# Residual block on one core: adaLN rows summed in two column halves, two stores moved later, S4's load moved ahead of the gate piece's

## The reference

```python
mod = silu(c) @ ada_w + ada_b                        # six rows of 1024: the adaLN rows
sh1, sc1, gt1, sh2, sc2, gt2 = split(mod, 6)
h = modulate(rmsnorm(x, pre_mix_g), sh1, sc1)
q_r, k_r, v_r, g_r, q_s, k_s, v_s, a_r, a_s = split(h @ w_in)
ret = silu(g_r) * groupnorm(retention(q_r, k_r, v_r, positions))   # 8 heads, chunks of 64 tokens
sb = stick_breaking(q_s, k_s, v_s)
mixed = sigmoid(a_r) * (ret @ w_ret_branch) + sigmoid(a_s) * (sb @ w_sb_branch)
x2 = x + gt1 * rmsnorm(mixed @ w_out, post_mix_g)
out = x2 + gt2 * rmsnorm(relu(modulate(rmsnorm(x2), sh2, sc2) @ w_ff1) ** 2 @ w_ff2)
```

## Time and profile before

| | us |
|---|---|
| runs, median (lowest to highest) | 1704.49 (1702.32 to 1706.66) |
| the profiled execution, own time | 1702.23 |
| its span | 1700.4 |
| TensorE busy | 1655.3 (97%) |
| DVE busy | 1048.7 (62%) |
| POOL busy | 753.5 (44%) |
| ACT busy | 661.6 (39%) |
| mean granted TensorE clock, 1 is full | 0.994 |

### The profile page before, as it was taken

The page is one execution under the profiler, slowest core; times in us unless marked ns, Lnnn a source line. Parts: engine busy times, 40 slices in busy tenths (PEclk is TensorE's granted clock), DMA queues, the critical chain, the costliest instruction groups (busy, mean ns, idle before and its releaser), DMA issues.

```text
span 1700.4 us, 25213 instructions
## 1 busy us (share of the span) xinstructions
PE 1655.3 (97%) x9680; PEld 1375.6 (81%) x9680; DVE 1048.7 (62%) x1350; ACT 661.6 (39%) x1130; POOL 753.5 (44%) x311
## 2 busy tenths in 40 slices
PE   5999999999998999999999999999999999999998
PEld 5887877777888898988888998787888888888876
DVE  6788788778346474942121557699664738383736
ACT  5566666210223243321001256435343444435352
POOL 2011111245534353523344752572767585858550
PEclk9999999999999999999999999999999999999999
DMA  9012121275835353423111444636684665748272
GB/s 355 21 70 81 41 85 65 93 280 194 337 125 213 137 188 114 152 100 149 50 49 49 162 166 157 222 137 231 244 330 172 272 239 217 285 166 341 99 293 99
DMA packets 62709, 288.32 MB, mean 170 GB/s; under 512 B 7956, under 2 KB 8852, under 8 KB 51992
## 3 DMA queue, kind: packets, MB, share of 16 engines
q1 hardware_dynamic: 50576, 258.57, 40.6%
q10 hardware_dynamic: 12040, 28.47, 4.6%
HBM read 249.25 MB, written 37.77 MB: 169 GB/s over the span
## 4 chain that ended last, share of the span: by engine, by line
PE 80%; DVE 9%; ACT 3%; issue 3%; DMA 3%; POOL 1%; SPq 0%; ACTq 0%; POOLq 0%; DVEq 0%
PE ps L872 8%; PE ps L874 8%; PE ps L873 7%; PE ps L1282 6%; PE ps L1284 6%; PE ps L1283 6%; PE ps L1327 4%; PE ps L1326 4%; PE ps L1325 4%; PE ps L958 4%; PE ps L959 4%; PE ps L960 4%; PE ps L1162 2%; PE ps L1011 2%; DVE fs_f L2388 2%
## 5 line engine op out<-in xcount | busy, mean ns | idle before, releaser
L1282 PE MATMUL ps<-w_hi,f_hi 128*128 128x512 f32 x440 | 175.3, 398 | 3.0 <-issue 2.7
L1284 PE MATMUL ps<-w_hi,f_lo 128*128 128x512 f32 x440 | 175.1, 398 | 0.0
L1283 PE MATMUL ps<-w_lo,f_hi 128*128 128x512 f32 x440 | 174.9, 397 | 0.0
L637 POOL TENSOR_TENSOR w_hi<-raw,zero 128x1024 fp32r<-128x1024 f32 x34 | 69.1, 2031 | 228.4 <-PE ps L874 113.4
L650 POOL TENSOR_TENSOR w_lo<-raw,w_hi 128x1024 fp32r<-128x1024 f32 x16 | 41.7, 2616 | 228.8 <-ACT w_hi L1405 202.1
L725 POOL TENSOR_TENSOR w_lo<-w,w_hi 128x1024 fp32r<-128x1024 f32 x34 | 84.7, 2496 | 112.2 <-ACT w_hi L1813 65.1
L1327 PE MATMUL ps<-ring,w_hi 128*128 128x512 f32 x336 | 134.0, 399 | 0.0
L1326 PE MATMUL ps<-ring,w_lo 128*128 128x512 f32 x336 | 132.4, 394 | 0.0
L1325 PE MATMUL ps<-ring,w_hi 128*128 128x512 f32 x336 | 131.8, 392 | 0.0
L2079 DVE TENSOR_TENSOR_SCAN uu<-uu 128x512 f32<-128x512 f32 (+7 forms) x96 | 100.0, 1083 | 37.5 <-ACT uu L1498 37.5
L667 POOL TENSOR_TENSOR w_lo<-raw,w_hi 128x1024 fp32r<-128x1024 f32 x24 | 59.7, 2492 | 132.6 <-ACT w_hi L1552 131.8
(11 more groups left out here) (300 smaller groups left out, 4801.4 us busy)
## 6 DMA issues: line engine op xcount, KB each, us to landing
ring<-ops SPq DMA_DIRECT2D x42, 2048.0 KB, 8.3
raw<-wstream SPq DMA_DIRECT2D x104, 512.0 KB, 3.5
ada_r<-ada_rows SPq DMA_DIRECT2D x32, 512.0 KB, 4.5
r_lo<-aops SPq DMA_DIRECT2D x16, 1024.0 KB, 5.3
r_hi<-aops SPq DMA_DIRECT2D x16, 1024.0 KB, 7.5
w<-wstream SPq DMA_DIRECT2D x32, 512.0 KB, 3.4
aops<-as_r ACTq DMA_DIRECT2D x16, 512.0 KB, 3.5
ada_s<-ada SPq DMA_DIRECT2D x7, 1024.0 KB, 16.8
```

Of the source, the lines that this page charges most:

```text
L1282: nc.tensor.matmul(bank, fh, wh, start=start, stop=False, skip_group_check=skip)
L1283: nc.tensor.matmul(bank, fh, wl, start=False, stop=False, skip_group_check=skip)
L1284: return nc.tensor.matmul(bank, fl, wh, start=False, stop=stop, skip_group_check=skip)
```

## The change

`ada_bank` gives the second half its row at partition 64 in place of 0, so the two matmuls of `ada_row` use different column halves of the array; ACT copies to the same partitions and stores a row with two DMAs of 2 KB, and the waits for these stores count to 8 instead of 4. In SP's list for each retention group, S4's load stands ahead of BGA's; in group 1 the store of `r` stands behind the loads of B22, S4, BGA and BGB instead of ahead of them. ACT's second store of `m1` stands behind the high part of BGB in group 0, instead of behind the group's second high part.

```diff
         def ada_bank(v, hv):
-            return px[0:1, (0, 2, 0, 0)[v] + hv, :]
+            return px[64 * hv:64 * hv + 1, (0, 2, 0, 0)[v] + hv, :]
...
                 sums_load(g, 1, gemm_done, tl + 4)
+                ret_load(1, g, B22, r_wsum, 4 * g + 4)
+                sums_load(g, 3, gemm_done, tl + 8)
+                ret_load(0, g, BGA, r_wlo, 9 * g + 5)
+                ret_load(1, g, BGB, r_wlo, 9 * g + 7)
                 if g == 1:
                     sp.wait_ge(r_lo_done, 4)
                     for part, r in enumerate((r_hi, r_lo)):
                         sp.dma_start(rsave[:, part, :, :], r[:, 0:2, :].bitcast(f32)).then_inc(rs_out, 16)
-                ret_load(1, g, B22, r_wsum, 4 * g + 4)
-                ret_load(0, g, BGA, r_wlo, 9 * g + 5)
-                sums_load(g, 3, gemm_done, tl + 8)
-                ret_load(1, g, BGB, r_wlo, 9 * g + 7)
                 if g + 1 < RET_G:
...
                 for hv in range(2):
-                    nc.scalar.activation(acc[0:1, v, hv, :], ada_bank(v, hv), ACT.Copy).then_inc(ada_ev, 1)
+                    nc.scalar.activation(acc[64 * hv:64 * hv + 1, v, hv, :], ada_bank(v, hv), ACT.Copy).then_inc(ada_ev, 1)
                 act.wait_ge(ada_ev, 2 + 2 * v + 2)
-                act.dma_start(mods[v:v + 1, :], acc[0:1, v, :, :].rearrange("p a n -> p (a n)")).then_inc(mods_out, 16)
+                for hv in range(2):
+                    act.dma_start(mods[v:v + 1, hv * HALF:(hv + 1) * HALF], acc[64 * hv:64 * hv + 1, v, hv, :]).then_inc(mods_out, 16)
...
                 ret_high(s3, raw[:, 0, :], (r_wsum, 4 * g + 2))
                 if g == 0:
-                    act.wait_ge(ev_dve, 8 * GATE_G)
-                    act.dma_start(m1_dram[:, 4:8, :], m1s[:, 4:8, :]).then_inc(m1_out, 16)
-                    act.wait_ge(mods_out, 16 * 4)
+                    act.wait_ge(mods_out, 16 * 8)
...
                 ret_high(s3, raw[:, 1, :], (ret_raw[1], 16 * (5 * g + 5)), (gemm_done, tl + 10))
+                if g == 0:
+                    act.wait_ge(ev_dve, 8 * GATE_G)
+                    act.dma_start(m1_dram[:, 4:8, :], m1s[:, 4:8, :]).then_inc(m1_out, 16)
                 for i in range(T):
...
-            dve.wait_ge(mods_out, 16 * 4)
+            dve.wait_ge(mods_out, 16 * 8)
```

## The result

The changed kernel takes 1708.4 us (median of 19 runs, 1703.49 to 1713.83) against 1703.77 for the kernel before (19 runs, 1702.06 to 1707.76) on the same chips: a ratio of 1.0028, 95% interval [1.002, 1.0037]. That is +4.7 us. The interval lies above 1, so it is a real slowdown, but it stays within the 0.3% (5.1 us) that the prediction counted as no change. The forecast was 1705.1, +0.6 on the median of the runs that it started from.

The account below looks back on a forecast made before the run. TensorE, busy for 97% of the span, was taken as the bound. The terms -2.6 - 5.5 - 9.1 + 12.0 + 5.8 gave +0.6 us, 1705.1 us on the median, range 1688 to 1712.

Parts of the forecast that it names:

- a late gate piece: Retention groups: BGA's later landing stalls TensorE's first gate products; forecast +0.6 us in all, chance 0.53 together with rival C.
- S4 ahead of BGA: All four retention groups: BGA lands behind S4, costing 12.0 us of TensorE stalls and 5.8 us of half clock.
- the chain of times: Group 2: BGA's high part at X + 9.1, DVE's rotation ending at X + 15.6, add 7 at X + 20.9.
- The stores: Retention groups 0 and 1: moving m1's store saves 5.5 us and r's store 9.1, waits and half clock gone.
- the price of 0 for their new places: Loads and POOL's sums held up behind the moved stores were to cost TensorE 0 us.
- Rival D: A store's new place makes a wait: POOL's sums for group 1 late for its first products; chance 0.03.
- rival C: Gate stage: the rows do not overlap, +2.6 us on the sum, 1708 us; chance 0.1.
- the prediction's other estimate: Gate stage rows: by the Trainium skill's share, two halves give 1.59 times, 0.65 us a row, 2.0 us.
- for three rows nothing else is close on TensorE: Gate stage: three rows each save TensorE 0.86 us with nothing else in the way, -2.6 us.
- The step for the fourth row: Before retention product 1: the fourth row gains nothing; TensorE arrives 0.86 us sooner and waits that much longer for S2.
- Rival A: Retention: the late gate piece is hidden, stalls under 1.3 us and the clock holds, 1687 to 1692 us; chance 0.27.
- B: Retention: the late gate piece costs more than both stores give back, stalls from 4 us, 1712 to 1716 us; chance 0.17.

Follow-up runs that it names:

- e4_s4_undone: The changed kernel with BGA's load ahead of S4's again in all groups: 1690.58 us, ratio 0.9916 against the kernel before.
- e1_rows: The kernel before with only the column halves for the adaLN rows: 1702.43 us against 1703.62, ratio 0.9992.
- e2_stores: The kernel before with both stores moved, S4 left behind BGA and the rows as before: 1692.09 us, ratio 0.9929.
- e10_act_highs_spread: e9 with two of DVE's row steps also moved behind the gate stage's first m1 products: 1687.91 us, ratio 0.9908 against the kernel before.
- e5_copies_first: The changed kernel with ACT's high part of BGA behind the two copies to `qk`: 1696.89 us, ratio 0.996 against the kernel before.
- e9: e4_s4_undone with ACT instead of POOL making the two high parts of retention group 0: 1688.16 us, ratio 0.9911 against the kernel before.

## Why the prediction was right, and where it was not

The number held (1708.4 within 1688 to 1712, "same" the likeliest), and the likeliest case was the one that came: a late gate piece that eats what the stores give. The size of +0.6 us was off by 4.1.

**S4 ahead of BGA.** Predicted 12.0 us of waits and 5.8 of clock, 17.8 in all; taken out of the changed kernel it gave 17.8. The halves of that sum were less exact than the whole. X is again the end of product 3. In the profile the four waits are 2.93, 1.81, 2.38 and 3.37, 10.5 us where 12.6 were named, and the clock fell behind two, not 3.5. In group 2 the chain of times itself was met within 0.1 us (high part, rotation, add 7), so what the step had wrong there is TensorE's own arrival: it came to the gate product at X + 18.6 (644.88 less 2.38 and 623.89), where the earlier trace rows had led to X + 18.0. In groups 0, 1 and 3 it came at X + 18.1, 19.4 and 18.3, where the earlier trace rows gave 17.76. Group 3 was the quickest case: in e4_s4_undone, with no wait there, the product came at X + 17.8 to 18.4. Waits and clock in the profiled execution make 10.5 and 2 x 1.65, that is 13.8 us, and not 17.8. From row 3 to that product at L872 it is 16.7 us longer than that of e4_s4_undone. Beside the 13.8 stand 1.2 us of waits on ACT's copies and 0.6 more at S2's load, which the sum did not have, and some 1.1 us are left. So the total met the forecast partly by luck.

**The stores.** Predicted -14.6, measured -11.5 (-12.1 by the ratio) together; both mechanisms held, and that they add. The half clock of the earlier trace rows in group 1 is gone, and the price of 0 for their new places was right: POOL's work for group 1 began 8.8 us later than the 476.73 of before, and no product waited for it.

```profile
485.54 2.38 POOL L656 TENSOR_TENSOR w_val<-raw 128x1024 f32<-128x1024 f32 x1 [12.87 <-DMA raw<-wstream]
```

Rival D is refuted by that. B22 took 5.4 us to land in group 0 and 7.8 in group 1, where about 6 was named for both.

**The rows.** This is the step that failed. The overlap is there (rival C is refuted: 0.86 us a row, to the decimal, and not the 0.65 of the prediction's other estimate), but "for three rows nothing else is close on TensorE" was wrong. In the profile that the prediction read, DVE's add was 1.7 us ahead of TensorE, and three rows took 2.6 us off TensorE's side. The rows of DVE and POOL for the gate stage were not read for their margin, only TensorE's waits; a margin shows in no list of waits. What it cost: -1.2 us in e1_rows and -1.5 us (e4_s4_undone against e2_stores) in place of -2.6. The interval of e1_rows, some -3.1 to +0.5 us, holds the -2.6 too, so the waits in the profiles show this and not the times. The step for the fourth row, eaten by S2's load, was right and too small: e10_act_highs_spread gave all of it back there, and more.

**Sum.** By the medians, from the kernel before to e2_stores -11.5, on to e4_s4_undone -1.5, on to the changed kernel +17.8: +4.8 us, against +4.7 measured and +0.6 forecast. Such a chain of kernels has to close, so its closing proves nothing; it gives the sizes. Of the 4.1 us between forecast and measurement, some 3.1 are the stores (or 2.5, by their ratio) and 1.1 the rows, whose intervals are as wide as that. Rival A did not come: neither ACT nor DVE got through, and e5_copies_first shows that with ACT's way cleared a third of the loss still stands. B did not either: the waits stayed below its 4 us.

## What to carry to other kernels

When TensorE is the bound and a change takes time out of it, read the other engines for how far ahead they are, because a list of waits shows only those that are already late, and read it in more than one profile: here the same add was 1.7 us early in one and 1.0 late in another with the same rows. A load that is swapped with a larger one costs through everything that stands behind its consumer in program order, and that can be more than the stores which were moved in the same change bring back; so time the parts of a change apart before keeping it. The version with both stores moved, the old order of S4 and BGA and ACT's high parts (1687.9 to 1688.2 us, e9 and e10) beats the kernel before by about 0.9% and the changed one by 1.2%; without ACT's high parts it is at 1690.6.

## What the runs showed of the hardware

- Two float32 products with one output column, in two column halves, overlap almost wholly: 1.88 us for four records became 1.03, and 0.86 us came off the step from row to row.
- DVE instructions with both large operands in SBUF get through about one for each of POOL's: 0.42 us became 2.5 and 2.6 beside two low parts (e5_copies_first). The adds that read one operand from PSUM were not held up beside POOL (0.69 us, at 636.24 in the changed kernel).
- The clock's fall does not follow the length of the last wait alone. Waits of 1.94 (before), 2.0 (e1_rows), 2.3 (e4_s4_undone), 2.73 (e10_act_highs_spread), 2.93 and 3.37 us (changed kernel) were followed by 1.2 GHz; in the changed kernel waits of 1.81, 1.96 and 2.38 were not, nor was the one of 3.11 us in the gate stage.
- No load on SP's queue landed ahead of one that was issued before it, in any of the 13 profiles (BGA behind S4 in group 2 of the changed kernel: 633.0 behind 631.7 us). The Trainium skill (DMA: Bandwidth & Descriptors, "Queues, rings and completion order") does not promise that; no row here shows the other way.
